# Down weights of a mixture of experts in column chunks: y block by block, in two banks

## The reference

```
t = rmsnorm(x) * (1 + sc2) + sh2                   # 288 x 2048
expert_id, top_w = top-1 group of 4, then top-2 of its 4 experts
a = einsum('nd,edf->enf', t, w_gate)               # 16 experts, 2048 x 512 each
b = einsum('nd,edf->enf', t, w_up)
hid = silu(a) * b * combine.T[:, :, None]          # combine: top_w, zero elsewhere
y = einsum('enf,efd->nd', hid, w_down)             # 512 x 2048 each
x = x + gt2 * y
out = rmsnorm(x, g_final)
```

## Time and profile before

| | |
|---|---|
| median of three runs | 1597.67 us |
| profiled execution, its own time | 1592.48 us |
| its span | 1590.7 us |
| PE busy | 1523.2 us (96%) |
| DVE, ACT, POOL busy | 591.5 us (37%), 482.0 us (30%), 250.6 us (16%) |
| HBM read | 452.93 MB |
| mean rate of the DMA engines | 287 GB/s |

### The profile page before, as it was taken

The page is one execution under the profiler, slowest core; times in us unless marked ns, Lnnn a source line. Parts: engine busy times, 40 slices in busy tenths (PEclk is TensorE's granted clock), DMA queues, the critical chain, the costliest instruction groups (busy, mean ns, idle before and its releaser), DMA issues.

```text
span 1590.7 us, 26816 instructions
## 1 busy us (share of the span) xinstructions
PE 1523.2 (96%) x10405; PEld 1181.9 (74%) x10405; DVE 591.5 (37%) x1020; ACT 482.0 (30%) x605; POOL 250.6 (16%) x408
## 2 busy tenths in 40 slices
PE   5889999999999999999999999999999999999995
PEld 2469999999899899898998999997445445445442
DVE  2333434434433344333343335545222222222225
ACT  2223333334333434434344334333011101101103
POOL 0005988701400000000000002443000000000002
PEclk9899999999999999999999999999999999999998
DMA  9997454542277665676765777425999999999993
GB/s 374 414 397 253 166 168 166 182 160 83 97 290 287 265 275 224 256 291 261 289 246 227 284 290 301 158 82 237 407 421 421 422 422 422 422 422 422 422 421 131
DMA packets 65525, 456.57 MB, mean 287 GB/s; under 512 B 7712, under 2 KB 8096, under 8 KB 12624
## 3 DMA queue, kind: packets, MB, share of 16 engines
q1 hardware_dynamic: 64768, 454.66, 71.7%
q0 software_dynamic: 720, 1.41, 0.3%
HBM read 452.93 MB, written 3.12 MB: 287 GB/s over the span
## 4 chain that ended last, share of the span: by engine, by line
PE 84%; DMA 11%; DVE 2%; issue 1%; ACT 1%; SPq 0%; DVEq 0%; ACTq 0%; PEldq 0%
PE bank L1309 18%; PE bank L1310 17%; PE bank L1311 17%; PE bank L1549 11%; PE bank L1615 6%; DMA ada<-in_w_ada 5%; PE bank L1255 5%; DMA dring<-in_w_down 3%; DMA ring<-in_w_up 3%; PE bank L1510 2%; PE bank L1531 1%; PE bank L1533 1%; PE bank L1246 1%; PE bank L1264 1%; PE bank L1559 1%
## 5 line engine op out<-in xcount | busy, mean ns | idle before, releaser
L850 DVE TENSOR_TENSOR wl<-mixw,wh 128x1024 fp32r<-128x1024 f32 x212 | 270.0, 1274 | 441.7 <-ACT wh L661 435.4
L1309 PE MATMUL bank<-hh,wh 128*128 128x288 f32 x1440 | 429.2, 298 | 1.4 <-DVE proj L850 1.4
L1310 PE MATMUL bank<-hl,wh 128*128 128x288 f32 x1440 | 425.6, 296 | 0.0
L1311 PE MATMUL bank<-hh,wl 128*128 128x288 f32 x1440 | 424.1, 294 | 0.0
L661 ACT ACTIVATE wh<-mixw 128x1024 fp32r<-128x1024 f32 x212 | 224.5, 1059 | 326.9 <-PE bank L1311 320.8
L1309 PEld LDWEIGHTS bank<-hh,wh 128*128 128x128 f32 x1440 | 270.5, 188 | 15.0 <-issue 14.9
L1311 PEld LDWEIGHTS bank<-hh,wl 128*128 128x128 f32 x1440 | 271.8, 189 | 0.0
L1310 PEld LDWEIGHTS bank<-hl,wh 128*128 128x128 f32 x1440 | 270.9, 188 | 0.1
L1549 PE MATMUL bank<-ring,xg 128*64 128x512 f32 x512 | 232.2, 597 | 4.9 <-DMA ring<-in_w_up 2.9
L1551 PE MATMUL bank<-ring,xg 128*64 128x512 f32 x512 | 232.6, 598 | 0.0
L1549 PEld LDWEIGHTS bank<-ring,xg 128*64 128x64 f32 x512 | 65.2, 136 | 126.1 <-issue 124.3
(11 more groups left out here) (278 smaller groups left out, 2085.0 us busy)
## 6 DMA issues: line engine op xcount, KB each, us to landing
adaw<-in_w_ada SPq DMA_DIRECT2D x64, 1024.0 KB, 5.7
ring<-in_w_gate SPq DMA_DIRECT2D x64, 1024.0 KB, 16.5
ring<-in_w_up SPq DMA_DIRECT2D x64, 1024.0 KB, 18.5
dring<-in_w_down SPq DMA_DIRECT2D x64, 1024.0 KB, 16.9
mixw<-in_w_gt SPq DMA_DIRECT2D x48, 1024.0 KB, 8.5
mixw<-in_w_mix SPq DMA_DIRECT2D x42, 1024.0 KB, 4.9
ada<-in_w_ada SPq DMA_DIRECT2D x32, 1024.0 KB, 16.1
brw<-in_w_br SPq DMA_DIRECT2D x16, 1536.0 KB, 9.5
```

The lines of the kernel that those rows point to most:

```text
L850: return dve.tensor_tensor(out, a, b, op)
L1309: mm(out, wh[:, s, k, :], hi[:, first + k, :], start=start and k == 0, stop=False)
L1310: mm(out, wh[:, s, k, :], lo[:, first + k, :], start=False, stop=False)
L1311: last = mm(out, wl[:, s, k, :], hi[:, first + k, :], start=False, stop=stop and k == HALF - 1)
```

## The change

A down load becomes one block of 512 columns of an expert: four pieces of 512 floats (2 KB) for each partition, one from each 128-row chunk. It has the form [128, 4, 512] of the other loads of the ring, and the name dring goes. PE takes y block by block: for block b all four chunks of both experts into bank 2 + b % 2. Behind block b (from 1 on) it scatters the two steps j = 2b - 2 and 2b - 1 of the block before, in the same pair; steps 6 and 7 of a pair stay beside the next pair's last `turn_gu`, and behind the last pair only they are left. A step j now covers the neighbouring tiles 2j and 2j + 1 of x, not j and 8 + j. Slots of down loads are released by `y_done`, so `moe_used` counts 16 for each pair (`slot_free`). Banks of the turns and gathers are dealt out anew, turns 6 and 7 come before the wait for mk and turn 8 alone between the rank matmuls and the sample rows; gather 3 waits until the last saves of the group before are done.

```diff
-        BANK_OF = (6, 7, 3, 4, 5, 2) * 2
-        GATHER_BANKS = (6, 7, 4, 5)
+        BANK_OF = (6, 7, 2, 4, 3, 5, 6, 2, 3, 7, 4, 5)
+        GATHER_BANKS = (1, 2, 3, 4, 5, 2, 3, 4)
...
                 else:
+                    blk = (c - 16) // 2
                     src = of_pair(w_down, n, c % 2, later).rearrange("m e (k p) n -> p (m e k) n", p=P)
-                    sp.dma_start(dring[k][:], src[:, (c - 16) // 2, :]).then_inc(slot_loaded[k], 16)
+                    sp.dma_start(ring8[k][:], src[:, :, 512 * blk:512 * blk + 512]).then_inc(slot_loaded[k], 16)
...
+            def slot_free(n, c, of=0, first=0, first4=0):
+
+                if c >= 12:
+                    sp.wait_ge(moe_used, first + n * 16 + (16 * of + c - 11))
+                elif c < 4:
+                    sp.wait_ge(moe_used, first + n * 16 + (16 * of + c - 3))
+                else:
+                    sp.wait_ge(y_done, first4 + n * 4 + (4 * of + (c - 4) // 2 - 3))
...
                 for p in range(2):
                     before = i * 16 + 8 * p
-                    for j in range(3):
-                        save_scat(j, before)
                     hidden(p, 0)
-                    for j in range(3, 6):
-                        save_scat(j, before)
+                    save_scat(6, before, 0)
                     hidden(p, 1)
-                    for j in (6, 7):
-                        save_scat(j, before)
+                    save_scat(7, before, 1)
...
                     for b in range(4):
                         dve.wait_ge(yhi_ready, i * 8 + (4 * p + b + 1))
-                        tt(ylo[:, 512 * b:512 * b + 512], bank[2 + b][:], yhi[:, 512 * b:512 * b + 512].bitcast(F32),
+                        tt(ylo[:, 512 * b:512 * b + 512], bank[2 + b % 2][:], yhi[:, 512 * b:512 * b + 512].bitcast(F32),
                            ALU.subtract).then_inc(ylo_ready, 1)
-                sample_rows(i + 2)
+                        if p == 1 and b == 3:
+                            sample_rows(i + 2)
+                        if b:
+                            for j in (2 * b - 2, 2 * b - 1):
+                                save_scat(j, before, 2 + j)
...
-            turn(range(1, 6))
+            turn(range(1, 8))
...
-            turn((6, 7))
+            turn((8,))
...
-            def scatter(j, before, total):
+            def scatter(j, sT_, total, k):
...
-                pe.wait_ge(acc_ready, total + max(j - 1, 0) + 1)
+                pe.wait_ge(acc_ready, total + (max(k, 1) + 5))
...
                     pe.wait_ge(hid_ready, i * EPG + (2 * p + 3))
-                    for c in range(FT):
+                    pe.wait_ge(st_ready, i * 2 + (p + 2))
+                    for b in range(4):
                         for e in range(2):
-                            k = (16 + 2 * c + e + 3) % 12
+                            k = (16 + 2 * b + e + 3) % 12
                             pe.wait_ge(slot_loaded[k], i * 64 + (32 * p + 32 + slot_uses(k)))
...
+                        if b >= 2:
+                            pe.wait_ge(ylo_ready, i * 8 + (4 * p + b))
+                        for k in range(FT):
                             for e in range(2):
...
+                                last = mm(bank[2 + b % 2][CAP * e:CAP * e + CAP, :], hid[e][:, k, :],
+                                          ring8[(16 + 2 * b + e + 3) % 12][:, k, :], start=k == 0, stop=k == FT - 1,
+                                          tile_position=(0, CAP * e))
+                        last.then_inc(y_done, 1)
+                        if b:
+                            pe.wait_ge(ylo_ready, i * 8 + (4 * p + b + 1))
+                            for j in (2 * b - 2, 2 * b - 1):
+                                scatter(j, sT[p], total, 2 + j)
+                sample_rows(i + 2)
...
-            for j in range(11):
-                if j < 8:
-                    scatter(j, 1, rounds * (8 * PAIRS))
...
+            for j in (6, 7):
+                scatter(j, sT[1], rounds * (8 * PAIRS), j - 6)
```

More of the change, by code:

```diff
@@ L803, in experts @@
                     act.activation(xg[:, 4 * q:4 * q + 2, :],
-                                   bank[GATHER_BANKS[2 * (q % 2)]].rearrange("p (a n) -> p a n", a=2), ACT.Copy).then_inc(xg_a, 1)
+                                   bank[GATHER_BANKS[2 * q]].rearrange("p (a n) -> p a n", a=2), ACT.Copy).then_inc(xg_a, 1)
                 for p in range(2):
                     for e in range(2):
-                        act.wait_ge(moe_used, i * (2 * PCH) + (PCH * p + 8 * e + 8))
+                        act.wait_ge(moe_used, i * 32 + (16 * p + 8 * e + 8))
                         if p == 0 and e == 0:
@@ L818, in experts @@
                         act.wait_ge(y_done, i * 8 + (4 * p + b + 1))
-                        act.activation(yhi[:, 512 * b:512 * b + 512], bank[2 + b][:], ACT.Copy).then_inc(yhi_ready, 1)
+                        act.activation(yhi[:, 512 * b:512 * b + 512], bank[2 + b % 2][:], ACT.Copy).then_inc(yhi_ready, 1)
             act.wait_ge(rounds_ready, 1)
@@ L827, in _ @@
             for j in range(8):
-                act.wait_ge(acc_ready, rounds * (8 * PAIRS) + (j + 2))
-                for f in (j, 8 + j):
+                act.wait_ge(acc_ready, rounds * (8 * PAIRS) + (j + 1))
+                for f in (2 * j, 2 * j + 1):
                     act.activation(sq4[:, f, :], x1[:, f, :], ACT.Square).then_inc(sq_ready, 1)
@@ L1218, in _ @@
             chain.loop(rounds, 16 * NG)
-            for j in range(8):
-                save_scat(j, rounds * (8 * PAIRS))
+            for j in (6, 7):
+                save_scat(j, rounds * (8 * PAIRS), j - 6)
             dve.wait_ge(sums_done, 5)
@@ L1463, in turn @@
                     if u >= 6:
-                        banks_read(BANK_OF[:u].index(BANK_OF[u]) + 1)
+                        v = BANK_OF[:u].index(BANK_OF[u])
+                        pe.wait_ge(thi_ready, v + 1)
+                        if v not in BY_GPSIMD:
+                            pe.wait_ge(tlo_ready, sum(w not in BY_GPSIMD for w in range(v + 1)))
                     for f in range(4):
@@ L1501, in _ @@
             sample_rows(1)
-            turn(range(8, 12))
-            def scatter(j, before, total):
+            turn(range(9, 12))
+            def scatter(j, sT_, total, k):
                 b = 4 + 2 * (j % 2)
-                pe.wait_ge(acc_ready, total + max(j - 1, 0) + 1)
+                pe.wait_ge(acc_ready, total + (max(k, 1) + 5))
                 for h in range(2):
+                    f = 2 * j + h
                     for part_, y in enumerate((yhi, ylo)):
-                        last = mm(bank[b + h][:, 0:T], y[:, P * (8 * h + j):P * (8 * h + j) + P], sT[before][:],
-                                  start=part_ == 0, stop=part_ == 1)
+                        last = mm(bank[b + h][:, 0:T], y[:, P * f:P * f + P], sT_[:], start=part_ == 0, stop=part_ == 1)
                 last.then_inc(scat_done, 1)
@@ L1602, in experts @@
                     last.then_inc(st_done, 1)
[L1603 removed]
+                    pe.wait_ge(tlp_ready, 2 * len(BY_GPSIMD) + 1)
+                    pe.wait_ge(ylo_ready, i * 8 + (4 * p + 1))
+                    scatter(6, sT[1 - p], total, 0)
                     turn_gu(p, 1)
[L1605 removed]
+                    scatter(7, sT[1 - p], total, 1)
                     pe.wait_ge(hid_ready, i * EPG + (2 * p + 3))
[L1607 removed]
+                    pe.wait_ge(st_ready, i * 2 + (p + 2))
@@ L1614, in experts @@
                             for e in range(2):
[L1615 to L1621, removed]
@@ L1633, in _ @@
             pe.wait_ge(ylo_ready, rounds * (4 * PAIRS) + 1)
-            for j in range(11):
-                if j < 8:
-                    scatter(j, 1, rounds * (8 * PAIRS))
-                if 3 <= j < 10:
-                    pe.wait_ge(sqs_ready, j - 3 + 2)
-                    mm(bank[0][:, 0:T], ones[:], sq4[:, j - 3, :], start=j == 3, stop=False)
-            for f in (7, 15):
-                pe.wait_ge(sq_ready, SQ_BEFORE + 15 + f // 8)
+            for j in (6, 7):
+                scatter(j, sT[1], rounds * (8 * PAIRS), j - 6)
+            for j in range(7):
+                pe.wait_ge(sqs_ready, j + 2)
+                mm(bank[0][:, 0:T], ones[:], sq4[:, 2 * j, :], start=j == 0, stop=False)
+            for f in (14, 15):
+                pe.wait_ge(sq_ready, SQ_BEFORE + 1 + f)
                 last = mm(bank[0][:, 0:T], ones[:], sq4[:, f, :], start=False, stop=f == 15)
```

66 lines of the change are left out of this document (24 added, 42 removed).

## The result

The changed kernel takes 1605.53 us (median of 17 runs, 1600.65 to 1608.38); the kernel before, run beside it, 1596.35 us (17 runs). The ratio is 1.0056, 95% interval 1.0044 to 1.0068: slower by 9.2 us, with 1604.3 us forecast and a range of 1593 to 1611.

What follows compares the result with a forecast made beforehand. The prediction took the expert stage's load stream as the bound, by a small margin over PE. Pieces +11.6, start -1.7 and tail -3.3 sum to +6.6 us on 1597.7, so 1604.3 us, range 1593 to 1611.

Steps and rivals of the forecast that it cites:

- The bound: Expert stage: the load stream at 422 GB/s ends it, by a small margin over PE; last down load lands at 1559.52 us.
- 2 KB pieces, +11.6: Down loads in the expert stage: each costs 0.182 us more in 2 KB pieces, 64 of them +11.6 us.
- mixq dips: Slower stretches around mix-weight loads of 2 KB pieces, 405 to 412 against 420 GB/s; mean 115 kB missing, used as the price.
- The doubt about the write side: Down loads: the price could be 0 if writing in pieces costs, since writes are contiguous here but not in mixq.
- Rivals 1 and 2: Down loads: no price for 2 KB pieces, 1592.7 us, chance 0.17; or half the price, 1598.5 us, chance 0.13.
- y in two banks, 0: PE's y blocks in the expert stage: new order, banks and waits cost 0 while the load stream is full.
- The pointer given for it: Sign of a right forecast in the expert stage: PE waits for down loads in nearly every pair.
- Start, -1.7: Start of the expert stage: turns 6 and 7 fill PE's idle time, second reload 1.7 us earlier (0 to -3).
- Tail, -3.3: From the last down load's landing to the end of the last squares: 12.6 us instead of 15.9 (0 to -6.7).
- The 15.2 us behind the squares stay: End of the kernel: the 15.2 us after the last squares were taken as unchanged.
- rival 4: Tail keeps its length, save 4 waiting behind sample rows and scatter 6 behind both saves: 1607.6 us, chance 0.05.
- The sum: Whole kernel: 11.6 - 1.7 - 3.3 = +6.6 us, added to a median of 1597.7 us for 1604.3.

Runs made afterwards that it cites:

- e1: Changed kernel with down weights laid out on the host so each load is one 8 KB run per partition: 1593.04 us, 0.9970 of the kernel before.
- e6: e1 with turns 6 and 7 put back behind the rank matmuls and 8 to 11 behind the sample rows: 1591.76 us, 0.9979 of the kernel before.
- e7: e1 with four of the seven column-sum matmuls put ahead of the last two scatters: 1591.16 us, 0.9962 of the kernel before.
- e4: Changed kernel with each down load in two pieces of 4 KB per partition, by host layout: 1599.25 us, 1.0026 of the kernel before.

## Why the prediction was right, step by step

**The bound.** Right: the load stream ends the stage, and the end moved with the rate. In after the last block of y still starts 0.09 us after the last down load has landed; counted from the first matmul behind the output projection that landing comes 11.9 us later than before, where about 10 was forecast. The margin on PE was as small as read from the earlier trace rows: once the loads are quick again (e1), PE ends the stage, 0.9 us behind the landing.

**2 KB pieces, +11.6.** Right in kind, too small: 64 x 0.218 = 14.0 by the rates, +13.7 by the traces. The mis-sized term is the price of one load, 0.182 us where 0.218 was measured. The missing bytes of the mixq dips were counted from 420 GB/s, a neighbouring window of the earlier trace rows, where the stage has 422. From 422 they are 136, 140 and 140 kB, 0.329 us for 1.5 MB and 0.219 us for 1 MB. That this is the reason is not shown: windows of 8 KB pieces alone beside the dips have 419 to 421 GB/s, so 420 was the fair level there. The rates are given in whole GB/s, and one of them over 14 us is 14 kB, a tenth of the dip: 0.182 and 0.219 were both inside what such rows can tell. The doubt about the write side is answered only so far: mixq is written in pieces and the down loads of after in one run of 8 KB, and their packets take the same time (88.1 and 88.7 ns), so pieces on the read side are enough. Pieces on the write side alone were not tried. Rivals 1 and 2 fall with this.

The rule of 512 B in the Trainium skill's "DMA: Bandwidth & Descriptors", section Specifications, does not hold for this stream: 410 GB/s with 2 KB, 417 with 4 KB, 422 with 8 KB, where a third of the loads has these pieces. The Trainium skill's "DMA: Bandwidth & Descriptors", section "Why small descriptors are slow (HBM only)", gives a fixed cost of about 3 cycles per packet beside one cycle per 32 bytes; an estimate by this figure of the Trainium skill is 67/64 against 259/256, 3.5% or 0.09 us per load at 2 KB and 0.03 at 4 KB. The direction agrees with these runs, the size is 2.5 to 3 times too small.

**y in two banks, 0.** Right: no wait of PE for a y eviction in the whole stage, and 422 GB/s in e1. The pointer given for it was half right: PE was to wait for down loads in nearly every pair. It does in four of eight, 3.6 us in all, and 23.5 us for gate and up loads. That costs nothing further, since the total is the stream's.

**Start, -1.7.** Right in size (-1.8) and in mechanism (e6). What is late next was only partly as put: DVE accounts for 0.28 us ahead of the sample rows and, by its copy of xg, for 0.5 us ahead of the first gate/up step, as forecast in kind. The largest new wait, 1.48 us ahead of the first gather, was not foreseen, and its cause stays open.

**Tail, -3.3.** The squares came as worked out: from the landing, 1574.95, to 1586.92 + 0.78 = 1587.70 it is 12.75 us, 12.6 forecast. The step that failed is "The 15.2 us behind the squares stay". They did not, because they held a condition: PE's column sums must be done by then. Before, they ran between the last scatters and behind them and were not late. Now all fourteen records stand behind two late scatters, on a PE that has just stood 3.3 us and runs at half clock. Of 3.1 us gained 1.5 were lost in this trace, 1.1 to 2.7 in the five with these sums; e7 gets them back. The wait that lets the clock fall is in rival 4 too (scatter 6 behind both saves), but there it was to hold up the squares, and these came on time.

**The sum.** +6.6 forecast, +10.3 by the traces, +9.2 by the runs: the stream 2.1 us more, the tail 1.7 less, the start as forecast. That 1604.3 came within 1.3 us of the median is in part luck: it was added to 1597.7, three runs of before, where the 17 beside after have 1596.35, and so a change 2.6 us too small met a start 1.3 us too high.

## What to carry to other kernels

A reshaped load pays for its pieces and not only for its bytes: on a stream that nothing hides, look in the same trace for a load of that form, and give the price that its dip yields a range as wide as the rounding of the rates. When data is wanted in another order and the host is free to lay it out, lay it out so in HBM (e1: the same columns, one piece per partition) rather than gather it in the DMA. A wait that a view puts down to `issue` or to a neighbour in time is looked up in the program, and against the landings, before anything is made of it. And a segment that is carried over as "stays the same" needs its inputs named: the sums behind the squares stayed only as long as PE came to them early and warm.

## What the hardware showed that was not expected

- A load of 1 MB read in 512 pieces of 2 KB cost 0.218 us more than in 128 of 8 KB, and in 256 of 4 KB 0.09 us by the rates, with all 16 DMA engines full either way; pieces 2 KB or 8 KB apart cost the same. A packet of 2 KB took 88.7 ns, of 4 KB 164.3, of 8 KB 313.8.
- SP's issue of a 1 MB load took 0.33 us (median) in one piece per partition and 2.4 us in four, and was not what the loss followed (2.0 us in e4).
- After 2.36 us (e6) and 3.32 us (after) in which PE stood, the clock was 0.50 while PE was at work again, and what that cost differed between executions (tails of 29.1 to 30.6 us with the same program); in e7, with gaps of 0.72 and 1.53 us in the same place, it stayed at 1.00.
- The same program part, 400 to 445 us, was granted 0.81 to 0.85 in some profiled executions and 0.96 in others, a difference of 3.5 us at the end: as much as start and tail brought together.
